# Last residual sums of a decoder layer on GpSimd in halves, with the root steps between them, and the samples' sum right behind its scale

## The chip, the cores and the metric

One core of one Trainium2 chip runs the whole kernel. The time is the device time of one execution in microseconds; below, PE is TensorE (matmul), DVE is VectorE, ACT is ScalarE, POOL is GpSimd, and SP is SyncE, which only issues DMAs here.

## The reference, cut to what matters

One layer of a hybrid decoder: retention and a causal convolution side by side, one output projection with a normalised residual, and a SwiGLU feed-forward net. There are 1,024 prompt tokens (8 tiles of 128 rows) and 8 sample tokens (one tile of 8 rows), each of width 1,024. What the change touches is the last line of the layer:

```python
def rms_norm(x, w):
    y = x32 * lax.rsqrt(jnp.mean(x32 * x32, axis=-1, keepdims=True) + EPS)
    return (y * w.astype(jnp.float32)).astype(x.dtype)
...
    h = h + rms_norm((jax.nn.silu(gate) * up) @ w_ffn_out, n_ffn_post)
```

So each row of the feed-forward output is squared and summed, scaled by a reciprocal root and a gain, added to `h`, and written out.

## The kernel before

The kernel is written instruction by instruction for each engine, and every order between engines is a semaphore. The feed-forward net runs over 11 groups of columns; its output gathers, transposed, in `ffn_acc`. The last group (`last_group`) is multiplied in 24 steps, and between them PE turns finished tiles back into rows of tokens.

The nine output tiles go in a fixed order, `LAST_ORDER = (5, 7, 3, 4, 6, 1, 8, 0, 2)`. Below a tile is named by its place in this order: order 0 to order 8. Order 6 is the tile of the 8 samples; all others have 128 rows. Orders 0 to 6 go through these steps:

1. PE transposes the tile into PSUM (L2161).
2. ACT squares it and sums each row (L1261).
3. DVE turns the sum into mean plus epsilon, `out_var` (L1701, one column). The semaphore is `s_var`.
4. POOL takes the power -0.5 of that column, `out_power` (L616). The semaphore is `s_rstd`.
5. DVE multiplies the tile by this scale and by the gain, `out_scale` (L1709). The semaphore is `s_fsc`.
6. `h_fin`, the residual, is added: for orders 0 to 5 by POOL in `out_add` (L825, semaphore `s_y`), for order 6 by DVE in its last instruction (L1777, `s_yd`).
7. SP stores the tile from `o_last` (L587).

Orders 7 and 8 go another way: PE multiplies the tile by a diagonal matrix of the gain (L2228), and one DVE instruction scales it and adds the residual (`out_finish`, L1719; order 8 in two halves of 512 columns). They still need steps 2 to 4.

Every engine executes its own list in order. POOL's list at the end is power 0, then for o from 0 to 4 the power of o+1 and the sum of o, then the powers 6, 7 and 8, and the sum of order 5. DVE's list behind its last product is `out_var` 6 and 7, `out_scale` 6, `out_var` 8, the three `out_finish` steps, and the sum of order 6. SP waits for each tile in the order 0, 1, 2, 3, 4, 7, the two halves of 8, then 5 and 6, and the program ends when all ten stores have landed.

Of the kernel before, what the change touches and what calls it, by code (L numbers as in the profile page):

```python
# [15 lines left out]
ALU = mybir.AluOpType  # L16
# [6 lines left out]
D = 1024  # L23
SEQ = 1024
META = 16
NS = 8
# [46 lines left out]
LAST_ORDER = (5, 7, 3, 4, 6, 1, 8, 0, 2)  # L73
# [16 lines left out]
def build(nc, x_prompt, x_sample, state_ret, state_conv, meta, n_mix_pre, n_mix_post, n_ffn_pre,  # L90
# [4 lines left out]
    with ctx:  # L95
        def at(name, shape, off, dt=F32):
            return nc.alloc_sbuf_tensor_at(name, shape, dt, offset=off)

        def sem(name):
            return ctx.enter_context(nc.semaphore(name))  # L100
# [16 lines left out]
        o_last = at("o_last", [P, 9, D], A)  # L117
# [44 lines left out]
        h_fin = [at(f"h_fin{t}", [P, D], A + 4096 * (9 + t) if t < 5 else B + 12 * tile_b + 4096 * (t - 5))  # L162
                 for t in range(9)]
# [93 lines left out]
        s_fT, s_fsc, s_y = (sem(n) for n in (  # L257
            "ffn_transposed", "ffn_scaled", "y_done"))
        s_yd, s_yout = sem("y_done_vector"), sem("y_out")
# [136 lines left out]
        def unit_chunks(un):  # L396
            return QG_CHUNKS if 8 <= un < 8 + H or un >= N_IN - H else IN_CHUNKS
# [28 lines left out]
        def rows_of(t):  # L426

            return META + NS if t == 0 else P
# [3 lines left out]
        def _(sp):  # L432
# [103 lines left out]
            for t in range(9):  # L536
                c0, n = OUT_TILES[t]
# [43 lines left out]
            for t in LAST_ORDER:  # L581
                c0, n = OUT_TILES[t]
                sp.dma_start(h_fin[t][0:n, :], h_scr[c0:c0 + n, :]).then_inc(s_tail, 16)
            def store(t, cols):
                c0, n = OUT_TILES[t]
                dst = y_prompt[0, c0:c0 + n, cols] if t < TILES else y_sample[:, 0, cols]
                sp.dma_start(dst, o_last[0:n, t, cols]).then_inc(s_yout, 16)  # L587

            for o in range(5):
                sp.wait_ge(s_y, o + 1)  # L590
                store(LAST_ORDER[o], slice(0, D))
            sp.wait_ge(s_yd, 1)
            store(LAST_ORDER[7], slice(0, D))
            for i in range(2):
                sp.wait_ge(s_yd, 2 + i)
                store(LAST_ORDER[8], slice(i * 512, (i + 1) * 512))
            sp.wait_ge(s_y, 6)
            store(LAST_ORDER[5], slice(0, D))
            sp.wait_ge(s_yd, 4)
            store(LAST_ORDER[6], slice(0, D))  # L600

            sp.wait_ge(s_yout, 10 * 16)
            for i in range(H):
# [6 lines left out]
        def _(pool):  # L610
            g = nc.gpsimd

            def power(dst, src, wait, count, done):

                pool.wait_ge(wait, count)
                g.tensor_tensor(dst, src, nhalf[0:src.shape[0], 0:src.shape[1]], ALU.pow).then_inc(done, 1)  # L616
# [4 lines left out]
            for t in range(9):  # L621
                n = rows_of(t)
# [17 lines left out]
            for j in range(24):  # L640
                un, c = divmod(j, 3)
                c0, n = unit_chunks(8 + un)[c]
# [44 lines left out]
            def x_sums_14(t):  # L687
                n = 4 if t == TILES else P
                _, _, xs = x_block(t)
                xa = x_rows(t, x_a[:, :, 0:n])  # L690
                pool.wait_ge(s_xs32, t // 2 * 2 + 2)
                g.tensor_tensor(xs[:, 20:24], xs[:, 16:20], xa[:, 0:4], ALU.add).then_inc(s_xs14, 1)
                g.tensor_tensor(xs[:, 24:28], xa[:, 4:8], xs[:, 16:20], ALU.subtract).then_inc(s_xs14, 1)
# [80 lines left out]
            for t in range(11):  # L774
# [4 lines left out]
                if t < 9:  # L779
                    n = OUT_TILES[t][1]  # L780
# [35 lines left out]
            def out_power(o):  # L816
                n, q = OUT_TILES[LAST_ORDER[o]][1], 96 + 3 * o
                power(st[0:n, q + 2:q + 3], st[0:n, q + 1:q + 2], s_var, 9 + o + 1, s_rstd)

            def out_add(o):  # L820
                t = LAST_ORDER[o]
                n = OUT_TILES[t][1]
                pool.wait_ge(s_tail, 9 * 16)
                pool.wait_ge(s_fsc, o + 1)
                g.tensor_tensor(o_last[0:n, t, :], o_last[0:n, t, :], h_fin[t][0:n, :], ALU.add).then_inc(s_y, 1)  # L825

            pool.wait_ge(s_gpre, 32)
            g.tensor_tensor(g_diag[:, :, :], g_last[:, :].rearrange("p (k n) -> p k n", k=KT),
                            ident.unsqueeze(1).to_broadcast([P, KT, P]), ALU.mult).then_inc(s_nh, 1)
            out_power(0)  # L830
            for o in range(5):
                out_power(o + 1)
                out_add(o)
            out_power(6)
            out_power(7)
            out_power(8)
            out_add(5)


        @block.scalar  # L840
        def _(act):
# [263 lines left out]
            def x_own(t):  # L1105

                xh, _, _ = x_block(t)
                n = 4 if t == TILES else P
                src = ps2[:, 3, :].rearrange("p (k n) -> p k n", k=KT)
                act.wait_ge(s_hT, t + 1)  # L1110
                if t % 2 == 0:
                    if t >= 2:
                        act.wait_ge(s_xs32, t)
                        act.wait_ge(s_xs14, t)
                    s.copy(x_a[:, :, 0:n], src[:, :, 0:n]).then_inc(s_xa, 1)
                    s.copy(xh[:, 0:8], x_rows(t, src if t == TILES else src[:, :, 0:n])).then_inc(s_fhi, 1)
                if t % 2 or t == TILES:
                    s.copy(xh[:, 8:12], x_rows(t, src[:, 4:8, :], False)).then_inc(s_fhi, 1)

            def x_sums_hi(t):  # L1120

                xh, _, xs = x_block(t)
                p2 = t // 2 * 2
                act.wait_ge(s_xs32, p2 + 2)
                s.copy(xh[:, 12:20], xs[:, 12:20]).then_inc(s_shi, 1)
                act.wait_ge(s_xs14, p2 + 2)
                s.copy(xh[:, 20:28], xs[:, 20:28]).then_inc(s_shi, 1)
# [138 lines left out]
        def _(dve):  # L1266
            v = nc.vector
# [212 lines left out]
            for n in range(TILES):  # L1480
# [19 lines left out]
                for hh in range(H):  # L1500
                    ins = v.scalar_tensor_tensor(out=R[:, (n + 1) % 2, hh, :], in0=R[:, n % 2, hh, :],
                                                 scalar=gam[hh] ** P, in1=ps[:, 4, hh * DH:(hh + 1) * DH],
                                                 op0=ALU.mult, op1=ALU.add)
# [3 lines left out]
                c0 = META + n * P  # L1507
# [190 lines left out]
            def out_var(o):  # L1698
                n, q = OUT_TILES[LAST_ORDER[o]][1], 96 + 3 * o
                dve.wait_ge(s_ss, 9 + o + 1)  # L1700
                v.tensor_scalar(st[0:n, q + 1:q + 2], st[0:n, q:q + 1], 1.0 / D, EPS,  # L1701
                                ALU.mult, ALU.add).then_inc(s_var, 1)

            def out_scale(o):
                t = LAST_ORDER[o]
                n, q = OUT_TILES[t][1], 96 + 3 * o
                dve.wait_ge(s_gpre, 32)
                dve.wait_ge(s_rstd, 9 + o + 1)
                v.scalar_tensor_tensor(out=o_last[0:n, t, :], in0=ps2[0:n, Y_PAIRS[o], :],  # L1709
                                       scalar=st[0:n, q + 2:q + 3],  # L1710
                                       in1=g_last[0:n, :], op0=ALU.mult, op1=ALU.mult).then_inc(s_fsc, 1)

            def out_finish(o, cols, count):
                t = LAST_ORDER[o]
                n, q = OUT_TILES[t][1], 96 + 3 * o
                dve.wait_ge(s_tail, 9 * 16)
                dve.wait_ge(s_rstd, 9 + o + 1)
                dve.wait_ge(s_xT, 9 + count)
                v.scalar_tensor_tensor(out=o_last[0:n, t, cols], in0=ps2[0:n, GAIN_PAIRS[o], cols],  # L1719
                                       scalar=st[0:n, q + 2:q + 3], in1=h_fin[t][0:n, cols],  # L1720
                                       op0=ALU.mult, op1=ALU.add).then_inc(s_yd, 1)
# [46 lines left out]
            out_var(6)  # L1768
            out_var(7)
            out_scale(6)  # L1770
            out_var(8)
            out_finish(7, slice(0, D), 1)
            out_finish(8, slice(0, 512), 2)
            out_finish(8, slice(512, D), 2)
            t = LAST_ORDER[6]
            dve.wait_ge(s_fsc, 7)
            v.tensor_tensor(o_last[0:NS, t, :], o_last[0:NS, t, :], h_fin[t][0:NS, :], ALU.add).then_inc(s_yd, 1)  # L1777


        @block.tensor  # L1780
# [508 lines left out]
```

## Time and profile before

| what | value |
|---|---|
| median of 3 runs | 1178.29 us (1177.98 to 1179.56) |
| the profiled execution, its own time | 1177.31 us |
| its span, first to last instruction | 1175.4 us |
| PE busy | 1148.9 us, 98% of the span |
| DVE busy | 802.2 us, 68% |
| POOL busy | 610.2 us, 52% |
| ACT busy | 444.3 us, 38% |
| mean granted TensorE clock | 0.993 of full speed |

The span is read from the trace; the time holds in addition what lies around the span, 1.9 us here. The busy shares are means over the whole span, and the change lies in the last 12 us of it, so they serve only to show which engine carries the rest.

### The profile page before, as it was taken

Reading aid. Unit: us, or ns where it says so; the run is one execution under the profiler, and the core shown is the slowest. Engines: PE = TensorE matmul, PEld = TensorE weight load, DVE = VectorE, ACT = ScalarE, POOL = GpSimd, SP = SyncE. Lnnn points to the kernel's source line nnn. Section 1 sums busy time; section 2 is a strip of 40 time slices with the busy share of each in tenths; the row PEclk is TensorE's granted clock in tenths of the full one; section 3 lists DMA queues with packets and bytes.
Section 4 is the critical chain, followed back from the end, with each engine's and each line's share of the span. In section 5 each row is a group of like instructions: output and inputs, shape, how many; then the busy total and the mean of one; then the engine's idle time right before and its main releaser. Section 6 shows DMA issues by size and latency. Waiting matters only on the chain.

```text
span 1175.4 us, 22876 instructions
## 1 busy us (share of the span) xinstructions
PE 1148.9 (98%) x8646; PEld 1129.1 (96%) x8646; DVE 802.2 (68%) x1242; ACT 444.3 (38%) x798; POOL 610.2 (52%) x455
## 2 busy tenths in 40 slices
PE   8999999999999999799999999999999999999997
PEld 7999999999999986699999999999999999999997
DVE  6368999954555247987685858584848585867646
ACT  6454454232334336642424233333333233333313
POOL 2066788304122357566565656474747473737316
PEclk9999999999989999899999999999999999999999
DMA  9311111111154223212121211212121212121134
GB/s 292 118 36 55 37 54 55 37 48 55 41 149 117 90 90 127 73 37 73 37 72 36 65 42 44 64 36 71 36 71 36 71 36 71 36 71 36 55 143 165
DMA packets 102360, 84.53 MB, mean 72 GB/s; under 512 B 2722, under 2 KB 89378, under 8 KB 102298
## 3 DMA queue, kind: packets, MB, share of 16 engines
q1 hardware_dynamic: 102258, 83.68, 23.2%
q8 instruction: 37, 0.61, 0.2%
q14 instruction: 17, 0.14, 0.0%
q10 hardware_dynamic: 48, 0.10, 0.0%
HBM read 72.86 MB, written 11.38 MB: 72 GB/s over the span
## 4 chain that ended last, share of the span: by engine, by line
PE 85%; DVE 5%; POOL 5%; issue 3%; DMA 2%; ACT 1%; DVEq 0%; SPq 0%; POOLq 0%; ACTq 0%
PE ps L409 26%; PE ps L411 26%; PE ps L410 26%; DVE w_ring L1601 1%; DMA f_raw<-in_w_ffn_in 1%; POOL o_last L825 1%; POOL h_ring L783 1%; PE ps L1965 1%; PE ps L1895 1%; PE ps L1914 1%; POOL st L616 1%; PE ps L2019 1%; PE ps L2018 1%; DMA x_st<-in_x_prompt 1%; DVE x_lo L1595 0%
## 5 line engine op out<-in xcount | busy, mean ns | idle before, releaser
L1737 DVE TENSOR_TENSOR ffn_acc<-ps,ffn_acc 128x516 f32<-128x516 f32 x264 | 183.6, 696 | 8.0 <-PE ps L411 2.6
L409 PE MATMUL ps<-xn_hi,w_hi 128*128 128x350 f32 (+2 forms) x576 | 187.2, 325 | 0.9 <-DVE xn_lo L1296 0.9
L411 PE MATMUL ps<-xn_lo,w_hi 128*128 128x350 f32 (+2 forms) x576 | 185.2, 322 | 0.0
L410 PE MATMUL ps<-xn_hi,w_lo 128*128 128x350 f32 (+2 forms) x576 | 184.9, 321 | 0.0
L409 PE MATMUL ps<-x_hi,w_ring 128*128 128x256 f32 x616 | 175.5, 285 | 5.8 <-DVE e_s L1615 3.8
L409 PE MATMUL ps<-x,w_ring 128*128 128x260 f32 x616 | 175.4, 285 | 1.6 <-issue 1.2
L410 PE MATMUL ps<-x,w_ring 128*128 128x260 f32 x616 | 175.3, 285 | 0.0
L411 PE MATMUL ps<-x,w_ring 128*128 128x260 f32 x616 | 175.0, 284 | 0.0
L410 PE MATMUL ps<-x_hi,w_ring 128*128 128x256 f32 x616 | 174.1, 283 | 0.0
L411 PE MATMUL ps<-x_lo,w_ring 128*128 128x256 f32 x616 | 174.1, 283 | 0.0
L409 PE MATMUL ps<-act_hi,w_ring 128*128 128x258 f32 x560 | 158.2, 283 | 0.1
L411 PE MATMUL ps<-act_lo,w_ring 128*128 128x258 f32 x560 | 157.8, 282 | 0.0
L410 PE MATMUL ps<-act_hi,w_ring 128*128 128x258 f32 x560 | 157.6, 281 | 0.0
L1601 DVE TENSOR_TENSOR w_ring<-f_raw,w_ring 128x512 fp32r<-128x512 f32 x135 | 102.8, 780 | 58.1 <-ACT w_ring L1143 57.1
L1143 ACT CAST w_ring<-f_raw 128x512 fp32r<-128x512 f32 x155 | 94.5, 619 | 118.0 <-POOL f_raw L730 83.9
L409 PEld LDWEIGHTS ps<-x_hi,w_ring 128*128 128x128 f32 x616 | 117.0, 190 | 7.6 <-DVE w_ring L1601 6.2
L409 PEld LDWEIGHTS ps<-x,w_ring 128*128 128x128 f32 x616 | 116.4, 189 | 2.1 <-issue 1.7
L411 PEld LDWEIGHTS ps<-x_lo,w_ring 128*128 128x128 f32 x616 | 117.2, 190 | 0.0
L410 PEld LDWEIGHTS ps<-x_hi,w_ring 128*128 128x128 f32 x616 | 117.2, 190 | 0.0
L410 PEld LDWEIGHTS ps<-x,w_ring 128*128 128x128 f32 x616 | 116.5, 189 | 0.0
L411 PEld LDWEIGHTS ps<-x,w_ring 128*128 128x128 f32 x616 | 116.4, 189 | 0.0
L1316 DVE SCALAR_TENSOR_TENSOR ps<-u,cw,ps 128x1024 f32<-128x1024 f32 x87 | 111.9, 1286 | 1.9
(257 smaller groups left out, 2672.4 us busy)
## 6 DMA issues: line engine op xcount, KB each, us to landing
f_raw<-in_w_ffn_in SPq DMA_DIRECT2D x42, 512.0 KB, 3.9
raw<-in_w_in SPq DMA_DIRECT2D x24, 512.0 KB, 3.9
f_raw<-in_w_ffn_out SPq DMA_DIRECT2D x22, 512.0 KB, 4.1
x_st<-in_x_prompt SPq DMA_DIRECT2D x8, 512.0 KB, 8.6
raw<-in_w_out SPq DMA_DIRECT2D x8, 512.0 KB, 6.6
h_ring<-in_x_prompt SPq DMA_DIRECT2D x8, 512.0 KB, 4.1
h_scratch<-h_ring SPq DMA_DIRECT2D x8, 512.0 KB, 3.1
h_fin<-h_scratch SPq DMA_DIRECT2D x8, 512.0 KB
```

Source lines behind the costliest of these rows:

```text
L409: nc.tensor.matmul(out, hi, mhi, start=first, stop=False, skip_group_check=resumes)
L410: nc.tensor.matmul(out, lo, mhi, start=False, stop=False, skip_group_check=resumes)
L411: return nc.tensor.matmul(out, hi, mlo, start=False, stop=last, skip_group_check=resumes)
L616: g.tensor_tensor(dst, src, nhalf[0:src.shape[0], 0:src.shape[1]], ALU.pow).then_inc(done, 1)
L783: g.tensor_tensor(h[t % 3][0:n, :], h[t % 3][0:n, :], m_sc[0:n, :], ALU.add).then_inc(s_h, 1)
L825: g.tensor_tensor(o_last[0:n, t, :], o_last[0:n, t, :], h_fin[t][0:n, :], ALU.add).then_inc(s_y, 1)
L1143: s.copy(w_slot(k, 0), w_op(k, first)).then_inc(s_ohi, 1)
L1316: v.scalar_tensor_tensor(out=win if w == 0 else tap_acc, in0=win, scalar=cw[:, ct, w:w + 1], in1=tap_acc, op0=ALU.mult, op1=ALU.add).then_ ...
L1601: v.tensor_tensor(w_slot(k, 1), w_op(k, first), w_slot(k, 0).bitcast(F32), ALU.subtract).then_inc(s_olo, 1)
L1737: v.tensor_tensor(a, tile_banks(i), a, ALU.add).then_inc(s_acc, 1)
L1895: ins = mm(ps[:, 4, hh * DH:(hh + 1) * DH], ins_k[0:rows, hh, :], ins_v[0:rows, hh, :], start=True, stop=True)
L1914: ins = mm(ps[:, 2, hh * P:(hh + 1) * P], kT[:, hh, c], qT[:, hh, c], start=True, stop=True)
```

## The change

POOL's sums of orders 4 and 5 are cut into halves of 512 columns. Its list ends power 5, first half of order 4, power 6, second half of order 4, power 7, first half of order 5, power 8, second half of order 5. On DVE the residual sum of the samples' tile (order 6) moves from the end to right behind `out_scale` 6, ahead of `out_var` 8 and the three `out_finish` steps; it waits for `s_fsc`, which `out_scale` 6 itself raises. SP's stores now come in the order 0, 1, 2, 3, 4, 6, 7, first half of 8, 5, second half of 8.

```diff
--- before.py
+++ after.py
@@ -590,14 +590,15 @@
                 sp.wait_ge(s_y, o + 1)
                 store(LAST_ORDER[o], slice(0, D))
             sp.wait_ge(s_yd, 1)
+            store(LAST_ORDER[6], slice(0, D))
+            sp.wait_ge(s_yd, 2)
             store(LAST_ORDER[7], slice(0, D))
-            for i in range(2):
-                sp.wait_ge(s_yd, 2 + i)
-                store(LAST_ORDER[8], slice(i * 512, (i + 1) * 512))
+            sp.wait_ge(s_yd, 3)
+            store(LAST_ORDER[8], slice(0, 512))
             sp.wait_ge(s_y, 6)
             store(LAST_ORDER[5], slice(0, D))
             sp.wait_ge(s_yd, 4)
-            store(LAST_ORDER[6], slice(0, D))
+            store(LAST_ORDER[8], slice(512, D))
 
             sp.wait_ge(s_yout, 10 * 16)
             for i in range(H):
@@ -817,24 +818,30 @@
                 n, q = OUT_TILES[LAST_ORDER[o]][1], 96 + 3 * o
                 power(st[0:n, q + 2:q + 3], st[0:n, q + 1:q + 2], s_var, 9 + o + 1, s_rstd)
 
-            def out_add(o):
+            def out_add(o, c0=0, c1=D):
                 t = LAST_ORDER[o]
                 n = OUT_TILES[t][1]
                 pool.wait_ge(s_tail, 9 * 16)
                 pool.wait_ge(s_fsc, o + 1)
-                g.tensor_tensor(o_last[0:n, t, :], o_last[0:n, t, :], h_fin[t][0:n, :], ALU.add).then_inc(s_y, 1)
+                ins = g.tensor_tensor(o_last[0:n, t, c0:c1], o_last[0:n, t, c0:c1], h_fin[t][0:n, c0:c1], ALU.add)
+                if c1 == D:
+                    ins.then_inc(s_y, 1)
 
             pool.wait_ge(s_gpre, 32)
             g.tensor_tensor(g_diag[:, :, :], g_last[:, :].rearrange("p (k n) -> p k n", k=KT),
                             ident.unsqueeze(1).to_broadcast([P, KT, P]), ALU.mult).then_inc(s_nh, 1)
             out_power(0)
-            for o in range(5):
+            for o in range(4):
                 out_power(o + 1)
                 out_add(o)
+            out_power(5)
+            out_add(4, 0, 512)
             out_power(6)
+            out_add(4, 512, D)
             out_power(7)
+            out_add(5, 0, 512)
             out_power(8)
-            out_add(5)
+            out_add(5, 512, D)
 
 
         @block.scalar
@@ -1768,13 +1775,13 @@
             out_var(6)
             out_var(7)
             out_scale(6)
+            t = LAST_ORDER[6]
+            dve.wait_ge(s_fsc, 7)
+            v.tensor_tensor(o_last[0:NS, t, :], o_last[0:NS, t, :], h_fin[t][0:NS, :], ALU.add).then_inc(s_yd, 1)
             out_var(8)
             out_finish(7, slice(0, D), 1)
             out_finish(8, slice(0, 512), 2)
             out_finish(8, slice(512, D), 2)
-            t = LAST_ORDER[6]
-            dve.wait_ge(s_fsc, 7)
-            v.tensor_tensor(o_last[0:NS, t, :], o_last[0:NS, t, :], h_fin[t][0:NS, :], ALU.add).then_inc(s_yd, 1)
 
 
         @block.tensor
```

## Rows read from the trace of the kernel before

**Rows 1.** The page of the profile, the chain that ended last, by engine.
```profile
PE 85%; DVE 5%; POOL 5%; issue 3%; DMA 2%; ACT 1%; DVEq 0%; SPq 0%; POOLq 0%; ACTq 0%
```

**Rows 2.** The same chain in order of time, its end (start us, us, what).
```profile
1166.12 0.49 POOL st L616
...
1166.71 0.92 DVE o_last L1709
...
1170.60 1.46 DVE o_last L1777
```

**Rows 3.** Timeline of POOL at the end (start us, us, engine, line, what).
```profile
1163.23 0.55 POOL L616 TENSOR_TENSOR st<-st,nhalf 128x1 f32<-128x1 f32 x1
1163.74 2.38 POOL L825 TENSOR_TENSOR o_last<-o_last,h_fin 128x1024 f32<-128x1024 f32 x1
1166.07 1.06 POOL L616 TENSOR_TENSOR st<-st,nhalf 8x1 f32<-8x1 f32 x2
1168.12 0.55 POOL L616 TENSOR_TENSOR st<-st,nhalf 128x1 f32<-128x1 f32 x1 [1.00 <-DVE st L1701]
1168.63 2.35 POOL L825 TENSOR_TENSOR o_last<-o_last,h_fin 128x1024 f32<-128x1024 f32 x1
```

**Rows 4.** Timeline of DVE, the same stretch.
```profile
1163.88 1.28 DVE L1709 SCALAR_TENSOR_TENSOR o_last<-ps,st,g_last 128x1024 f32<-128x1024 f32 x1 [0.85 <-POOL st L616]
...
1165.08 0.13 DVE L1701 TENSOR_SCALAR st<-st 8x1 f32<-8x1 f32 x1
...
1165.83 0.15 DVE L1701 TENSOR_SCALAR st<-st 128x1 f32<-128x1 f32 x1 [0.62 <-ACT sq_last L1261]
...
1166.71 1.27 DVE L1709 SCALAR_TENSOR_TENSOR o_last<-ps,st,g_last 8x1024 f32<-8x1024 f32 x1 [0.72 <-POOL st L616]
...
1167.91 0.13 DVE L1701 TENSOR_SCALAR st<-st 128x1 f32<-128x1 f32 x1
...
1167.97 2.63 DVE L1719 SCALAR_TENSOR_TENSOR o_last<-ps,st,h_fin 128x1024 f32<-128x1024 f32 x3
...
1170.52 1.55 DVE L1777 TENSOR_TENSOR o_last<-o_last,h_fin 8x1024 f32<-8x1024 f32 x1
```

**Rows 5.** Timeline of SP's queue, four of the last stores as issued.
```profile
1169.26 0.33 SPq L587 DMA_DIRECT2D out<-o_last  x1
...
1170.63 0.33 SPq L587 DMA_DIRECT2D out<-o_last  x1
...
1171.02 0.56 SPq L587 DMA_DIRECT2D out<-o_last  x1
...
1172.09 0.30 SPq L587 DMA_DIRECT2D out<-o_last  x1
```

**Rows 6.** Busy time by stretch; the last two columns are DMA's share and GB/s.
```profile
1169.50:1170.00 0.50, 0.00 (x0) 0.00 (x0) 0.50 (x2) 0.00 (x0) 0.50 (x1) 1.00 0.00 0
1170.00:1174.00 4.00, 0.00 (x0) 0.00 (x0) 2.06 (x2) 0.00 (x0) 0.99 (x1) 0.84 1.00 389
1174.00:1174.50 0.50, 0.00 (x0) 0.00 (x0) 0.00 (x0) 0.00 (x0) 0.00 (x0) 0.50 0.57 98
```

**Rows 7.** Groups of instructions by form, POOL and DVE (count, busy us, mean ns).
```profile
L722 POOL TENSOR_TENSOR f_raw<-f_raw 128x512 f32<-128x512 f32 x31 | 40.7, 1312 | 0.0
...
L1657 DVE TENSOR_TENSOR fx_lo<-f_raw,fx_hi 128x1024 fp32r<-128x1024 f32 x2 | 2.4, 1216 | 0.0
```

**Rows 8.** Timelines of POOL and of DVE from 948.7 to 952 us.
```profile
948.76 1.31 POOL L737 TENSOR_TENSOR act_lo<-e_s,act_hi 128x516 fp32r<-128x516 f32 x1
...
950.02 1.75 POOL L737 TENSOR_TENSOR act_lo<-x_diff,act_hi 128x516 fp32r<-128x516 f32 x1
...
949.37 1.25 DVE L1601 TENSOR_TENSOR w_ring<-f_raw,w_ring 128x512 fp32r<-128x512 f32 x1 [1.75 <-ACT w_ring L1143]
```

**Rows 9.** Timelines of POOL and of DVE around 475 us.
```profile
474.76 0.99 POOL L616 TENSOR_TENSOR st<-st,nhalf 8x1 f32<-8x1 f32 x1
...
473.78 2.17 DVE L1601 TENSOR_TENSOR w_ring<-t_first,w_ring 128x512 fp32r<-128x512 f32 x2 [0.36 <-ACT w_ring L1143]
```

## The prediction

> **What bounds the kernel now.** I read the chain that ended last first. PE carries 85% of it, and none of PE's work is touched [rows 1]; DVE and POOL have 5% each. In order of time the chain then shows where PE lets go: at the end it runs over POOL's root steps, `out_scale` 6 and the last sum on DVE [rows 2]. So at most the last 12 us are at stake.
>
> The timelines show why POOL is in this chain. It adds order 4 from 1163.74 for 2.38 us, while `out_var` 6 is ready at 1165.08 + 0.13 and `out_var` 7 at 1165.83 + 0.15; powers 6 and 7 start only at 1166.07 [rows 3, 4]. `out_scale` 6 therefore starts at 1166.71. Then DVE is busy without a gap to 1172.07, while POOL idles for 1.0 us ahead of power 8 [rows 3, 4].
>
> The chain names the sum of order 6 as its last work, but the stores decide differently. The store of order 7 is issued at 1169.26; the DMA engines move nothing from 1169.5 to 1170.0, then run full (share 1.00, 389 GB/s) until 1174.0 [rows 5, 6]. That is the 1.57 MB of order 7, both halves of order 8, and order 5 (three tiles of 0.524 MB): 1.57 MB / 389 GB/s = 4.0 us. The store of the samples, 32 KB issued at 1172.09, only stands behind them [rows 5]. **The end is a drain: it begins 0.75 us after the store of order 7 is issued and takes 4.0 us, as long as the next store is always there in time.** From its end to the span's end at 1175.4 lie 1.4 us, in the first 0.5 of which 0.05 MB still move [rows 6].
>
> **The change part by part.**
>
> *First half of order 4, then power 6.* A half has 512 columns; POOL's sums of 128x512 take 1.31 us [rows 7]. 1163.74 + 1.30 = 1165.04. A power starts 0.21 us after its `out_var` starts (1167.91 to 1168.12), and a scale 0.65 us after its power (1163.23 to 1163.88) [rows 3, 4]. So power 6 starts at 1165.08 + 0.21 = 1165.29 and `out_scale` 6 at about 1165.95: 0.76 us earlier. It ends at 1167.22.
>
> *The split itself.* Two halves cost 2.6 us where one sum costs 2.38 [rows 3, 7], 0.2 us of POOL per tile. The store of order 4 becomes ready at 1167.1 instead of 1166.12: second half 1165.80 to 1167.10. It costs nothing: those bytes take 1.35 us and are through before the drain starts. If DMA were still busy, it would push the drain by what is left.
>
> *Power 7* now stands behind that half: 1167.06 to 1167.61, instead of done at 1167.13 [rows 3]. DVE doesn't ask for it until `out_finish` 7, below, so this is covered by the moved sum.
>
> *The samples' sum on DVE.* It is the one part that costs on the path: ahead of `out_finish` 7 stands an instruction more. Both its inputs lie in SBUF, like L1657, which takes 1.22 us for the same 1,024 columns [rows 7]; at the end it took 1.55 [rows 4], ending 1.09 us after POOL's sum ended (1168.63 + 2.35 = 1170.98) [rows 3]. Such instructions of the two engines exclude each other in this trace: at 949.37 a DVE instruction waits for POOL's and ends 0.55 after it, and POOL's next one, which started at once, takes 1.75 instead of 1.31 [rows 8]. So DVE takes its turn where POOL passes from one instruction to the next, and POOL pays then, ending 1.15 us after DVE. Rows 8 show one of nine such places, all alike, between 585 and 1071 us.
>
> The sum can start at 1167.22. POOL's power 7 runs then, to 1167.61. The three possible prices:
> - the power does not hold DVE: the sum ends at 1168.44. Rows 9 lean this way: two DVE instructions of 512 columns are through at 475.95, 1.15 us after POOL's previous sum ended at 474.80, undelayed beside a power [rows 9];
> - it holds it: 1167.61 + 1.09 = 1168.70;
> - DVE comes first and holds the power: there the power takes 0.99 instead of 0.54, ending 0.4 after DVE. Then power 7 ends at 1168.85 and `out_finish` 7, which needs it, starts at 1168.95.
>
> `out_var` 8 and `out_finish` 7 follow. `out_finish` 7 started at 1167.97 [rows 4]; now at 1168.44, 1168.70 or 1168.95, that is +0.47, +0.73 or +0.98. I take the middle, +0.73. The Trainium skill (SBUF — State Buffer, "SBUF: two separate sides") says that VectorE with two SBUF inputs and a GpSimd instruction hold their shared port pair exclusively, for the whole instruction, and the loser fully blocks. Rows 8 agree; taken to the letter for the power too, it gives the +0.73, while rows 9 let DVE pass.
>
> *What POOL does after that.* The first half of order 5 is queued behind the samples' sum: 1168.70 + 1.15 = 1169.85. Power 8, which ended at 1168.67 [rows 3], is behind it: 1169.82 to 1170.37. The halves of order 8 wait for it on DVE: 1170.48 to 1171.22 and to 1171.90. The second half of order 5 runs 1170.34 to 1171.64. So the very wait the change takes from power 6 comes back at power 8, which now comes 1.7 us later.
>
> *The stores.* Order 7 is issued at 1169.26 + 0.73 = 1169.99, its data run from 1170.73 to 1172.08. The first half of 8 is issued at 1171.25, data possible from 1172.00: just in time, 0.08 us to spare. Order 5 at 1171.68 (from 1172.43; needed at 1172.75), the second half of 8 at about 1172.24 (from 1173.0; needed at 1174.1). The drain has no hole and ends at 1170.73 + 4.0 = 1174.77 instead of 1174.03: +0.73. The samples' store, 32 KB, moves out of it into idle DMA time at about 1169; between nothing and the 0.3 us in which the last 0.05 MB crept [rows 6] are saved: 0.15 taken.
>
> Sum: +0.73 - 0.15 = **+0.6 us**. Bounds: +0.47 - 0.3 = +0.2 to +0.98 - 0 = +1.0, and up to 0.4 more if the first half of 8 arrives late behind a held power. The profiled execution would have a span of 1176.0 and a time of 1177.9; it lies 0.98 us below the median shown, which therefore becomes 1178.29 + 0.6 = **1178.9 us**.
>
> **The rivals.** A measurement of this kernel can tell 0.2%, 2.4 us, from no change.
>
> *POOL keeps its turn (slower).* If the first half of order 5 starts ahead of the samples' sum, DVE waits for 1167.57 + 1.30 = 1168.87, the sum ends at 1169.96 and the store of order 7 is issued 2.0 us later: +1.8 us, 1180.1. Against it: both engines start from power 6, POOL needs 1.30 + 0.55 us until then, DVE 1.27; and at each boundary like rows 8 DVE got its turn. It decides on a slower only if order 7's store goes out more than 2.5 us later, after 1171.8; that takes 0.5 us beyond this. Chance 0.12.
>
> *The last store's own way sets the end.* If the 3.3 us from the samples' issue at 1172.09 to 1175.4 are a fixed way and no queue, the end follows the last issue: 1172.24 instead of 1172.09, with a store of 0.26 MB: -0.3 to +0.2 us, 1178.2. The Trainium skill (DMA: Bandwidth & Descriptors, "Anatomy of one DMA") gives a fixed cost of about 2.0 us per DMA, most of it the receipt of the write; that is less than the 3.3 us here. Against it: the full DMA share until 1174.0 [rows 6]. Chance 0.2.
>
> *The change frees what it names.* If power 8 came early too and the drain were limited by order 5 being ready late, the end would move by up to 0.76 us forward: 1177.5. Against it: order 5's data are needed only after those of 7 and 8. Chance 0.06.
>
> My forecast (+0.2 to +1.0, 1178.5 to 1179.3) has 0.57; 0.05 is left for what no row shows. All these cases lie within 0.2%. The range of 8 in 10 takes in the first rival and the last, and the spread of the three runs shown (-0.3 to +1.3): 1177.4 to 1180.4. Faster 0.04, same 0.89, slower 0.07, the last from the first rival's far end.
>
> **What would show it.** Right: power 6 near 1165.3 and `out_scale` 6 near 1165.95; the samples' sum right behind it, 1.2 to 1.5 us; the first half of order 5 longer than 1.31 us by the wait; power 8 after 1169.5; DMA full for 4.0 us from about 1170.7; span 1176.0. Wrong: `out_finish` 7 at 1168.0 or before (the sum hidden), at 1169.9 (POOL kept its turn), a hole in the drain between 7 and 8, or an end that does not follow the drain.

## The result, and the profile after

| | median | runs |
|---|---|---|
| before | 1178.89 us | 20 |
| the change | 1180.93 us | 20 |

The ratio is 1.0015, 95% interval 1.0008 to 1.0022: the change costs 1.8 us (0.9 to 2.6). It is slower, clear of the noise, by an amount whose middle value stays below the 0.2% of the prediction. The ratio leaves out one run of each kernel that took far longer (1874 and 6380 us). The median shown for the kernel before had been 1178.29 over 3 runs; over 20 it is 1178.89.

Where the extra lies can't be read from the two spans. Before it is 1175.4, after 1179.6, but 2.7 of these 4.2 us arise before `out_var` 6, and the change moves nothing that `out_var` 6 waits for: it starts at 1165.08 before [rows 4] and at 1167.81 after. Over the 15 executions profiled in this study it started between 1164.0 and 1167.8, with the same DVE instructions ahead of it. So all that follows is counted from the start of `out_var` 6, by three marks: **A**, to the start of `out_finish` 7; **S**, to the issue of order 7's first store; **Z**, to the end of the span (two decimals of Z use the span as the trace holds it, to 0.001 us).

The timelines of DVE and then of POOL in the changed kernel (start us, us):

```profile
1167.81 0.13 DVE L1708 TENSOR_SCALAR st<-st 8x1 f32<-8x1 f32 x1
...
1168.66 1.27 DVE L1716 SCALAR_TENSOR_TENSOR o_last<-ps,st,g_last 8x1024 f32<-8x1024 f32 x1
1169.97 2.65 DVE L1780 TENSOR_TENSOR o_last<-o_last,h_fin 8x1024 f32<-8x1024 f32 x1
1172.55 0.14 DVE L1708 TENSOR_SCALAR st<-st 128x1 f32<-128x1 f32 x1
1172.61 2.58 DVE L1726 SCALAR_TENSOR_TENSOR o_last<-ps,st,h_fin 128x1024 f32<-128x1024 f32 x3
```

```profile
1168.02 0.54 POOL L617 TENSOR_TENSOR st<-st,nhalf 8x1 f32<-8x1 f32 x1 [0.27 <-DVE st L1708]
1168.53 1.26 POOL L826 TENSOR_TENSOR o_last<-o_last,h_fin 128x512 f32<-128x512 f32 x1
1169.77 0.54 POOL L617 TENSOR_TENSOR st<-st,nhalf 128x1 f32<-128x1 f32 x1
1170.28 1.25 POOL L826 TENSOR_TENSOR o_last<-o_last,h_fin 128x512 f32<-128x512 f32 x1
1172.76 0.55 POOL L617 TENSOR_TENSOR st<-st,nhalf 128x1 f32<-128x1 f32 x1 [1.22 <-DVE st L1708]
```

To be seen, against [rows 3, 4]: power 6 and `out_scale` 6 come as early as forecast, 0.21 and 0.85 us after `out_var` 6 (before 0.99 and 1.63). Then the samples' sum stands on DVE for **2.65 us** instead of 1.2 to 1.5. It ends at 1172.62, which is 1.09 us after POOL's half of order 5 ended (1170.28 + 1.25 = 1171.53), the same 1.09 as at the end of the kernel before. And that half takes 1.25 us, not stretched at all: it was POOL that had the turn. `out_finish` 7 starts 4.80 us after `out_var` 6 instead of 2.89, and POOL idles 1.22 us ahead of power 8.

The DMA engines in the same kernel, by stretch (the last two columns are their share and GB/s), around the drain:

```profile
1174.20:1174.60 0.40, 0.00 (x0) 0.00 (x0) 0.40 (x2) 0.00 (x0) 0.34 (x1) 1.00 0.00 0
1174.70:1178.70 4.00, 0.00 (x0) 0.00 (x0) 0.49 (x1) 0.00 (x0) 0.00 (x0) 0.73 1.00 392
1178.70:1179.20 0.50, 0.00 (x0) 0.00 (x0) 0.00 (x0) 0.00 (x0) 0.00 (x0) 0.50 0.05 12
```

The drain is there as before [rows 6]: nothing, 4.0 us at full share, next to nothing. It begins 0.8 us after order 7's store is issued at 1173.90 (S 6.10). What differs is its end. Before, it took 6.16 us from that issue to the end of the span (Z 10.34 - S 4.18); here 5.69 (11.79 - 6.10). The samples' 32 KB, which had come last and now come ahead of the drain, had cost 0.47 us at its tail.

### The profile page after: what moved, and what is told of

Same layout as the page of the kernel before. It is cut to its first block, busy times and chain, and to the rows that moved or that the text cites. A ratio compares the mean times of both kernels' runs of the same rounds, so it can differ in the third digit from the quotient of the medians.

```text
span 1179.6 us, 22880 instructions
## 1 busy us (share of the span) xinstructions
PE 1151.0 (98%) x8646; PEld 1131.3 (96%) x8646; DVE 803.2 (68%) x1242; ACT 444.3 (38%) x798; POOL 610.8 (52%) x457
## 4 chain that ended last, share of the span: by engine, by line
PE 85%; DVE 5%; POOL 4%; issue 3%; DMA 2%; ACT 1%; DVEq 0%; SPq 0%; POOLq 0%; ACTq 0%
PE ps L409 26%; PE ps L411 26%; PE ps L410 26%; DVE w_ring L1608 2%; DMA f_raw<-in_w_ffn_in 1%; PE ps L1972 1%; POOL o_last L826 1%; POOL h_ring L784 1%; POOL st L617 1%; PE ps L1902 1%; PE ps L1921 1%; PE ps L2026 1%; PE ps L2025 1%; DMA x_st<-in_x_prompt 1%; DVE x_lo L1602 0%
## 5 line engine op out<-in xcount | busy, mean ns | idle before, releaser
L617 POOL TENSOR_TENSOR st<-st,nhalf 128x1 f32<-128x1 f32 (+4 forms) x54 | 33.8, 628 | 155.3 <-DVE st L1501 68.9
```

## The experiments

Marks in us, each from one profiled execution; ratios are to the kernel before on the same chip, with their 95% intervals. "Sum" is the duration of the samples' residual sum on DVE. "Split" is the cutting of POOL's sums into halves.

| kernel | sum | A | S | Z | Z - S | ratio |
|---|---|---|---|---|---|---|
| before | 1.55 | 2.89 | 4.18 | 10.34 | 6.16 | |
| the change | 2.65 | 4.80 | 6.10 | 11.79 | 5.69 | 1.0015 (1.0008 to 1.0022) |
| the change again | 2.65 | 4.81 | 6.10 | 11.82 | 5.72 | 1.0019 (1.0009 to 1.0029) |
| split only | 1.20 | 2.59 | 3.90 | 10.06 | 6.16 | 0.9998 (0.9987 to 1.0008) |
| sum only | 1.21 | 4.16 | 5.45 | 11.14 | 5.69 | 1.0007 (0.9998 to 1.0015) |
| nothing behind power 7 | 1.21 | 3.36 | 4.65 | 10.34 | 5.69 | 0.9995 (0.9985 to 1.0005) |
| power 7 ahead of the half | 1.69 | 3.84 | 5.13 | 10.81 | 5.68 | 1.0000 (0.9989 to 1.0010) |
| sum from PSUM | 1.21 | 3.36 | 4.65 | 10.34 | 5.69 | 1.0004 (0.9991 to 1.0016) |
| split 384/640 | 1.21 | 3.87 | 5.18 | 10.87 | 5.69 | 1.0012 (1.0002 to 1.0023) |
| wait for power 7 | 1.21 | 3.36 | 4.66 | 10.35 | 5.69 | 1.0000 (0.9990 to 1.0010) |
| before, stores swapped | 1.54 | 2.89 | 4.18 | 10.58 | 6.40 | 0.9999 (0.9989 to 1.0009) |
| before, no samples' sum | none | 2.89 | 4.18 | 9.90 | 5.72 | 1.0000 (0.9987 to 1.0012) |
| one split, stores swapped | 1.21 | 2.59 | 3.90 | 10.26 | 6.36 | 1.0002 (0.9993 to 1.0011) |
| the same, order 7 in halves | 1.21 | 2.60 | 3.38 | 10.08 | 6.70 | 0.9998 (0.9987 to 1.0008) |
| halves, samples last | 1.21 | 2.59 | 3.37 | 9.76 | 6.39 | 0.9991 (0.9981 to 1.0001) |

The ratios alone are too wide to separate half a microsecond; the marks repeat to 0.03 us where the same code ran again (A and S of the kernel before, in three kernels; all marks of the change, in two).

### Which part costs

The split alone. POOL as in the change; on DVE and SP the order of before:

```diff
             out_scale(6)
-            t = LAST_ORDER[6]
-            dve.wait_ge(s_fsc, 7)
-            v.tensor_tensor(o_last[0:NS, t, :], o_last[0:NS, t, :], h_fin[t][0:NS, :], ALU.add).then_inc(s_yd, 1)
             out_var(8)
...
             out_finish(8, slice(512, D), 2)
+            t = LAST_ORDER[6]
+            dve.wait_ge(s_fsc, 7)
+            v.tensor_tensor(o_last[0:NS, t, :], o_last[0:NS, t, :], h_fin[t][0:NS, :], ALU.add).then_inc(s_yd, 1)
```

> POOL's halves and root steps as in the change, the samples' sum back at DVE's end, stores in the order of before. Two marks are read from the profile: A, from the start of out_var 6 to the start of out_finish 7 (2.89 us before, 4.80 in the change), and Z, from the start of out_var 6 to the end of the span (10.3 before, 11.8 in the change). Theory 1 (the moved sum is what costs, because it waits behind power 7 and then behind the first half of order 5): A 2.6, Z 10.1, time 0.2 us under the kernel before. Theory 2 (the split costs, because power 8 stands behind a half and tears a hole into the drain): Z 11 or more, time about that of the change.

A 2.59, Z 10.06: 0.28 us less than before. The split does what it says, and its late power 8 tears no hole.

The sum alone. DVE and SP as in the change, POOL's list as before:

```diff
-            for o in range(4):
+            for o in range(5):
                 out_power(o + 1)
                 out_add(o)
-            out_power(5)
-            out_add(4, 0, 512)
             out_power(6)
-            out_add(4, 512, D)
             out_power(7)
-            out_add(5, 0, 512)
             out_power(8)
-            out_add(5, 512, D)
+            out_add(5)
```

> Only the samples' sum moved, POOL's list as before. Theory 1: POOL has nothing to do while the sum runs, so it takes its bare 1.22 us instead of 2.65; out_scale 6 is as late as before; A 4.2, Z 11.5, ratio 1.001. Theory 2 (split): A and Z as before, 2.9 and 10.3. Theory 3 (the sum is slow in this place whatever POOL does): it takes 2.6 us, A 5.6, Z 12.9.

The sum takes its bare 1.21 us, A 4.16 as forecast, and Z 11.14, 0.8 us more than before (11.5 was forecast; the samples' store, moved ahead of the drain, gave 0.47 back). It is the moved sum that costs; but 1.44 us of its 2.65 need the split as well. The two parts together (+1.45) cost more than one after the other (+0.80 - 0.28).

The changed kernel once more:

> The changed kernel itself, once more. If the samples' sum waits behind the first half of order 5 by the order of the lists and not by chance: it takes 2.65 us again, A 4.8, Z 11.8, ratio 1.001 to 1.0015. If it was chance: the sum takes 1.2 to 1.5 us, A 3.4 to 3.9.

The same to 0.03 us, ratio 1.0019. So the wait comes with the kernel, not by chance.

### What the samples' sum waits for

Both halves of order 5 put behind power 8:

```diff
             out_power(7)
-            out_add(5, 0, 512)
             out_power(8)
+            out_add(5, 0, 512)
             out_add(5, 512, D)
```

> The change, but both halves of order 5 behind power 8, so that nothing waits in POOL's list behind power 7 when the samples' sum comes. Theory 1: the sum takes 1.2 to 1.5 us instead of 2.65, A 3.4 to 3.9, Z 10.5 to 10.9, about 1 us under the change. 1.22 us would say that a power does not hold DVE at all, 1.5 that it does. Theory 3 (slow in this place whatever is queued): 2.6 us, A 4.8, as in the change.

The timelines of DVE and of POOL:

```profile
1169.33 1.21 DVE L1780 TENSOR_TENSOR o_last<-o_last,h_fin 8x1024 f32<-8x1024 f32 x1
```

```profile
1169.14 0.54 POOL L617 TENSOR_TENSOR st<-st,nhalf 128x1 f32<-128x1 f32 x1
```

The sum takes 1.21 us. It starts 0.2 us after power 7 as in the change, and power 7 takes its usual 0.54: this power holds DVE not at all. Z is 10.34, the same as before and less than the 10.5 to 10.9 that was forecast: the bare sum puts 0.47 us on the path, and the samples' store, out of the drain, gives 0.47 back. So without the wait the change would have been worth nothing in either direction.

The sum reads PSUM in place of `o_last` (this kernel leaves out the samples' scale and gain; the length and the place of the instruction stay):

```diff
-            v.tensor_tensor(o_last[0:NS, t, :], o_last[0:NS, t, :], h_fin[t][0:NS, :], ALU.add).then_inc(s_yd, 1)
+            v.tensor_tensor(o_last[0:NS, t, :], ps2[0:NS, Y_PAIRS[6], :], h_fin[t][0:NS, :], ALU.add).then_inc(s_yd, 1)
```

> The change, but the samples' sum reads the unscaled tile from PSUM instead of o_last, so only one of its inputs lies in SBUF (the samples come out without scale and gain; the length of the instruction and its place stay). Theory 1 (what costs is the exclusion between a DVE instruction with two SBUF inputs and POOL's): it takes 1.2 us though the first half of order 5 runs beside it, A 3.4, Z 10.3. Rival (DVE is held by something else, its semaphore or the 8 rows): 2.65 us, A 4.8.

The timelines of DVE and of POOL:

```profile
1168.63 1.21 DVE L1780 TENSOR_TENSOR o_last<-ps,h_fin 8x1024 f32<-8x1024 f32 x1
```

```profile
1168.95 1.26 POOL L826 TENSOR_TENSOR o_last<-o_last,h_fin 128x512 f32<-128x512 f32 x1
```

1.21 us, with the half of order 5 beside it in the same place as in the change. So the 1.44 us are the exclusion between POOL's half and a DVE instruction with both inputs in SBUF; with one input in PSUM it is gone, though the semaphores and the rows are the same.

### Who gets the turn

Power 7 ahead of the second half of order 4, so that DVE asks while a sum runs (here the half of order 4) and another stands behind it:

```diff
             out_power(6)
-            out_add(4, 512, D)
             out_power(7)
+            out_add(4, 512, D)
             out_add(5, 0, 512)
```

> The change, but power 7 ahead of the second half of order 4, so that the samples' sum comes while a sum of POOL runs and another sum stands behind that. If DVE gets its turn where one POOL sum passes to the next, as in the steady state: the sum takes 1.6 to 1.7 us, the first half of order 5 is stretched from 1.25 to about 1.7 or more, A 3.8. If POOL keeps its turn here too: the sum takes 2.9 us, no POOL instruction is stretched, A 5.1.

DVE gets its turn: 1.69 us, ending 1.08 after POOL's half of order 4. POOL's next half is stretched. POOL's timeline has both halves in one row, 3.48 us for what takes 2 x 1.27 alone:

```profile
1167.01 0.55 POOL L617 TENSOR_TENSOR st<-st,nhalf 128x1 f32<-128x1 f32 x1 [0.23 <-DVE st L1708]
1167.53 3.48 POOL L826 TENSOR_TENSOR o_last<-o_last,h_fin 128x512 f32<-128x512 f32 x2
```

Order 4 cut at 384 columns, so that the samples' sum comes just before a POOL sum ends and power 7 is next:

```diff
-            out_add(4, 0, 512)
+            out_add(4, 0, 384)
...
-            out_add(4, 512, D)
+            out_add(4, 384, D)
```

> The change, with order 4's sum cut at 384 instead of 512 columns: its second part then ends at about 2.3 us after out_var 6, and the samples' sum comes at 2.16, while a POOL sum runs and power 7 is next. If the one who asks while a sum runs gets the turn at its end: the samples' sum takes 1.2 to 1.3 us and power 7 is held to the sum's end, about 3.8, so A is 3.9, Z 10.9. If what stands in POOL's list behind a power always goes ahead: the sum waits for power 7 and the first half of order 5, takes 2.9 us, A 5.1, Z 12.0.

POOL's timeline:

```profile
1164.74 1.54 POOL L826 TENSOR_TENSOR o_last<-o_last,h_fin 128x640 f32<-128x640 f32 x1
1166.24 1.55 POOL L617 TENSOR_TENSOR st<-st,nhalf 128x1 f32<-128x1 f32 x1
1167.77 1.26 POOL L826 TENSOR_TENSOR o_last<-o_last,h_fin 128x512 f32<-128x512 f32 x1
```

The sum (1166.17, 1.21 us) is not delayed, and **power 7 takes 1.55 us instead of 0.54**, ending 0.41 after it; `out_finish` 7 waits for that, A 3.87, which is 0.98 more than before: the third price of the prediction, to the hundredth. A power was held by DVE here, where it stands behind a sum of POOL at whose end DVE had its turn; it was not held in the change and in the two kernels above, where it had started before DVE asked.

Left open by these: why POOL's half goes ahead of DVE behind a power, and what POOL has next does not behind a sum. One wait more tells a part of it:

```diff
             out_power(7)
+            pool.wait_ge(s_rstd, 9 + 8)
             out_add(5, 0, 512)
```

> The change with one wait more: POOL waits for power 7's own semaphore before it issues the first half of order 5. Open is why that half goes ahead of the samples' sum, which asks 0.3 us before the half's record starts. If the half has claimed the port while power 7 still runs (it is in POOL's pipeline already): with the wait it can't, the samples' sum takes 1.2 us, the half starts or ends behind it, A 3.4, Z 10.3, ratio 1.000. If POOL has the turn behind a power in any case: the sum takes 2.65 us or 0.1 more, A 4.8 to 4.9, Z 11.8, ratio 1.0015.

The timelines of POOL and of DVE:

```profile
1167.56 0.54 POOL L617 TENSOR_TENSOR st<-st,nhalf 128x1 f32<-128x1 f32 x1
1168.18 1.94 POOL L826 TENSOR_TENSOR o_last<-o_last,h_fin 128x512 f32<-128x512 f32 x1
```

```profile
1167.77 1.21 DVE L1781 TENSOR_TENSOR o_last<-o_last,h_fin 8x1024 f32<-8x1024 f32 x1
...
1168.98 1.26 DVE L1727 SCALAR_TENSOR_TENSOR o_last<-ps,st,h_fin 128x1024 f32<-128x1024 f32 x1
```

Power 7 is still in front and DVE asks at the same point, 2.16 after `out_var` 6. Now it has the turn: 1.21 us, and it is the half that is stretched, to 1.94. The wait costs POOL 0.10 us of start (0.62 after power 7's, not 0.52) and gives back 1.44 on the path. So it is not enough that the half of order 5 stands behind a power. What the runs leave is that, unless it is made to wait, it has its claim to SBUF in while the power still runs: ahead of a DVE instruction whose record starts 0.32 us before the half's own (2.16 against 2.48). The records don't show the claim; it is inferred from who waits. Nor do they show how early it is made, and why there is none behind a sum: with order 4 cut at 384, power 7's record starts only 0.07 us after DVE's, and DVE still goes first. The ratio of the kernel with the wait is 1.0000.

The kernel before has a place of the same kind, long before its end. The timelines of POOL and of DVE there:

```profile
389.28 0.25 POOL L662 TENSOR_TENSOR mix<-ys,mix 128x32 fp32r<-128x32 f32 x1
389.50 1.28 POOL L719 TENSOR_TENSOR t_first<-f_first 128x512 f32<-128x512 f32 x1
```

```profile
389.49 2.37 DVE L1453 TENSOR_TENSOR mix<-gT,mix 128x1024 fp32r<-128x1024 f32 x1 [0.80 <-ACT mix L979]
```

A small instruction of POOL (32 columns, 0.25 us), a sum-sized one right behind it, and a DVE instruction with both inputs in SBUF that asks while the small one runs, by its record 0.01 us ahead of the large one. DVE takes 2.37 us for 1,024 columns and ends 1.09 us after POOL's large instruction. The two starts are nearly even here, so this row doesn't prove the order; but it is what the prediction needed to look at, a passage from a small instruction to a large one, and there POOL kept its turn.

### What sets the end

The kernel before with SP's last stores in another order:

```diff
-            for i in range(2):
-                sp.wait_ge(s_yd, 2 + i)
-                store(LAST_ORDER[8], slice(i * 512, (i + 1) * 512))
+            sp.wait_ge(s_yd, 2)
+            store(LAST_ORDER[8], slice(0, 512))
             sp.wait_ge(s_y, 6)
             store(LAST_ORDER[5], slice(0, D))
             sp.wait_ge(s_yd, 4)
             store(LAST_ORDER[6], slice(0, D))
+            store(LAST_ORDER[8], slice(512, D))
```

> The kernel before, with nothing changed but the order of SP's last stores: order 5, then the samples' 32 KB, then the second half of order 8 (it was the samples' that came last). So far the end of the span followed the issue of order 7's store by 6.16 us in the two kernels whose last store is the samples' and by 5.69 in the four where it stands earlier. Theory 1 (the end is a drain that starts with order 7's store, and the samples' 8 rows, when they come last, cost 0.47 us more than a store of 128 rows): Z 9.9 instead of 10.34, A as before at 2.9, time 0.5 us less. Rival (the end follows the last issue): the last issue comes 0.4 us later than before, Z 10.7 or more.

A miss for theory 1: Z 10.58, 0.24 more than before. Nor did the rival's 10.7 come; from the last issue to the end are 3.24 us here, 3.33 before, 4.02 in the change and 3.97 in the kernel without the sum, so the end does not follow it. The stretches at the end of this drain:

```profile
1172.60:1175.60 3.00, 0.00 (x0) 0.00 (x0) 1.98 (x2) 0.00 (x0) 0.91 (x1) 1.00 1.01 403
1175.60:1176.10 0.50, 0.00 (x0) 0.00 (x0) 0.00 (x0) 0.00 (x0) 0.00 (x0) 1.00 1.34 320
1176.10:1176.60 0.50, 0.00 (x0) 0.00 (x0) 0.00 (x0) 0.00 (x0) 0.00 (x0) 1.00 0.64 234
1176.60:1177.10 0.50, 0.00 (x0) 0.00 (x0) 0.00 (x0) 0.00 (x0) 0.00 (x0) 0.82 0.49 184
```

It runs at 403 GB/s for 3.0 us, and then, with the samples' rows in it, falls to 320, 234 and 184: a 0.26 MB store behind them is drawn out with them. Measured against the 5.69 us of Z - S with the samples' store ahead of the drain, it costs 0.47 us as the last and 0.7 in the middle.

The kernel before without the samples' residual sum (the samples come out without their residual), their store ahead of order 7's:

```diff
+            sp.wait_ge(s_fsc, 7)
+            store(LAST_ORDER[6], slice(0, D))
             sp.wait_ge(s_yd, 1)
             store(LAST_ORDER[7], slice(0, D))
...
-            sp.wait_ge(s_yd, 4)
-            store(LAST_ORDER[6], slice(0, D))
```

> The kernel before without the samples' residual sum (the samples come out without their residual), their store ahead of order 7's. Theory: the sum at DVE's end was covered by the drain and costs nothing there, and the store costs nothing ahead of the drain: A 2.9 as before, order 7's store issued at 4.2, Z 4.18 + 5.69 = 9.9. Rival (the sum at the end was on the path): Z 9.4 or less, since it took 1.5 us.

Z 9.90, as forecast to 0.03: 1.55 us of work taken from the end of DVE's list, and only the store's 0.44 us come back. The sum that the chain of waits names as its last work was covered by the drain.

### Versions

One split, powers 7 and 8 next, order 5 whole, the samples' sum at the end, stores swapped:

```diff
             out_add(4, 512, D)
             out_power(7)
-            out_add(5, 0, 512)
             out_power(8)
-            out_add(5, 512, D)
+            out_add(5)
```

> A version from what was found: only order 4's sum in halves around power 6, powers 7 and 8 next, order 5's sum whole, the samples' sum at DVE's end, the samples' store ahead of order 8's second half. Theory 1: A 2.6, order 7's store issued 3.9 us after out_var 6, Z 3.9 + 5.69 = 9.6, 0.7 us under the kernel before. Rival (order 5 becomes the late one, since its sum now comes behind power 8): Z 10.3 or more.

S 3.90 as forecast, Z 10.26 instead of 9.6: the miss is the swapped stores again.

The same with order 7 in halves:

```diff
-            out_finish(7, slice(0, D), 1)
+            out_finish(7, slice(0, 512), 1)
+            out_finish(7, slice(512, D), 1)
```

> As the version with one split and the stores swapped, and out_finish 7 in two halves of 512 columns, each with its own store, so that the drain can start after the first half. Theory 1: the first half's store is issued at 3.35, Z 9.05 to 9.35 (up to 0.3 us of hole, since the samples' store is ready only at 6.7), 1.0 to 1.3 us under the kernel before. Rival (the drain's start is not what sets the end): Z 9.6 as without the halves.

S 3.38; Z 10.08 instead of 9.05 to 9.35, for the same reason.

The halves kept, and the stores put as 7, 7, 8, 8, 5 and the samples last (order 8's second half moves up behind its first; against the kernel just above):

```diff
...
-            sp.wait_ge(s_yd, 3)
-            store(LAST_ORDER[8], slice(0, 512))
...
+            for c in range(2):
+                sp.wait_ge(s_yd, 3 + c)
+                store(LAST_ORDER[8], slice(c * 512, (c + 1) * 512))
             sp.wait_ge(s_y, 6)
...
             store(LAST_ORDER[6], slice(0, D))
-            store(LAST_ORDER[8], slice(512, D))
```

> The three versions with the samples' store inside the drain and another behind it ended later than theory 1 said: the end followed the first issue of order 7 by 6.4 us (stores swapped) where 5.69 was forecast, against 6.16 with the samples last. So the samples' store costs least ahead of the drain (5.69), more as its last (6.16), most in its middle (6.4). This kernel keeps order 7's two halves and puts the stores as 7, 7, 8, 8, 5, and the samples last: first issue at 3.38, Z 3.38 + 6.16 = 9.5 to 9.6, 0.75 us under the kernel before, ratio 0.9994. Rival (order 7's halves give nothing, since SP's issues or the first half of 8 then leave a hole): Z 10.0 or more.

Z 9.76, 0.58 us under the kernel before and the best of those that leave nothing out; 0.2 us above the forecast. Order 8's first half is issued at 4.89 as ever, while order 7's bytes are now through sooner, which is the likely reason; it was not tried apart. The ratio, 0.9991 (0.9981 to 1.0001), does not exclude no change.

## Why the prediction was wrong

The time lies 0.5 us above the range of 8 in 10, and what was given as likeliest, +0.6 us (+0.2 to +1.0), was +1.8 (0.9 to 2.6) by the ratio and +1.45 by Z.

**The failing step** is in "The samples' sum on DVE": "So DVE takes its turn where POOL passes from one instruction to the next". Rows 8 show this where a sum of POOL passes to a sum, and it was applied to the passage from power 7 to the half of order 5. There it doesn't hold: the half goes first, and DVE waits until it is through. The step gave +0.73 for the start of `out_finish` 7; it measured +1.91. That is the rival "POOL keeps its turn", priced at +1.99 for the start of `out_finish` 7 and given 0.12. What was held against it, that POOL needs 1.30 + 0.55 us until the half and DVE 1.27, compared the starts of two records; the half's record does start later, by 0.32 us, and the half still went first.

**The second error** is the size of the samples' store: 0.15 taken, between 0 and 0.3; it measured 0.47 (0.44 without the sum). 1.91 - 0.47 = 1.44, the difference of Z (1.45). The rival with its own numbers, +1.8, would have been 0.35 too high by Z, 0.32 of it from the store.

Of the other steps:
- *Power 6 and `out_scale` 6, 0.76 us earlier:* 0.78. Right. Alone, with the sum left at the end, this is worth 0.28 at the end, because `out_var` 8, which stands ahead of `out_finish` 7, then waits 0.36 us for ACT's last square.
- *The split's 0.2 us and order 4's later store cost nothing:* right (split only, Z 10.06).
- *The three prices:* where nothing stands behind the power, the first (+0.47, the power does not hold DVE) is what came: A 3.36 against 2.89. The middle price, +0.73, which I took and which the Trainium skill (SBUF — State Buffer, "SBUF: two separate sides") gives if a power counts as a GpSimd instruction like others, did not occur; for POOL's larger sums the runs agree with its rule that the loser waits for the whole instruction (the samples' sum stretched to 1.69 and 2.65 us, POOL's half to 1.94). Its rule that the one that starts first gets the ports does not come out by the starts of the records: DVE's was 0.32 us earlier, and DVE lost.
- *The end is a drain of 4.0 us that starts with order 7's store:* right in every kernel whose samples' store is outside the drain: Z - S is 5.68 to 5.72 over nine profiles in which S runs from 4.18 to 6.10.
- *The last store's own way sets the end:* refuted. The 2.0 us that the prediction sets beside it from the Trainium skill (DMA: Bandwidth & Descriptors, "Anatomy of one DMA") stand there for a DMA issued by GpSimd, while these stores are issued by SP; no sum used them.
- *The baseline:* the range was missed by 0.53 us, and the median of before moved by 0.60 when it was taken over twenty runs. Without this shift the time would have come out at 1180.3, inside the range, with the same step wrong: the range reached up to +2.1 because it took in the rival. With the centre right, at +1.8, the shift would not have mattered.

## What to carry to other kernels

A DVE instruction with both inputs in SBUF should not be put where POOL has a sum queued behind a tiny instruction: here DVE waited until that sum was through. A wait of POOL for its own tiny instruction, or one operand in PSUM, gave the 1.4 us back. And where the end is a drain of stores, what counts is the issue of the first large store. Work in front of it costs in full; work behind it cost nothing here as long as the next store was issued in time; and a small store of few rows belongs ahead of the drain, not within it.

## What the runs showed of the hardware

- POOL's sum of 128x512 went ahead of a DVE instruction with two SBUF inputs whose record starts 0.32 us before its own, when the POOL instruction in front was one of one column (0.54 us); not when it waited for that one's semaphore, and not when a sum of 512 columns was in front. Where DVE lost, it ended 1.09 us after POOL's sum; where POOL lost, its half ended 1.13 us after DVE.
- A one-column POOL instruction that had started 0.2 us before did not delay a DVE instruction with two SBUF inputs (1.21 us). One that came 0.07 us behind such an instruction was held by it: 1.55 us instead of 0.54.
- A store of 8 rows of 4 KB cost 0.47 us at the end of a full drain and 0.7 ahead of its last 0.26 MB, in which the rate falls from 403 to 184 GB/s; why such rows are that slow was not tried.
